# Two transformer blocks on one core: routing on unscaled rows, three weight loads issued earlier, the first expert's gate and up products apart

## The reference, cut to what matters

```python
hn = rmsnorm(h, norm_ffn[i])
tokens = hn.reshape(-1, d)
g_logits = tokens @ w_router_group
g_probs = jax.nn.softmax(g_logits, axis=-1)
g_idx = jnp.argmax(g_logits, axis=-1)
g_w = jnp.take_along_axis(g_probs, g_idx[:, None], axis=1)
e_logits = jnp.einsum("nd,gde->nge", tokens, w_router_expert)
e_sel = jnp.take_along_axis(e_logits, g_idx[:, None, None], axis=1)[:, 0]
top_v, top_i = lax.top_k(e_sel, TOP_K_IN_GROUP)
gates = g_w * jax.nn.softmax(top_v, axis=-1)
...
def run_block(args):      # xb: the tokens of expert e
    xb, e = args
    return (jax.nn.silu(xb @ w_gate[e]) * (xb @ w_up[e])) @ w_down[e]
...
out = jnp.zeros((n, d), jnp.float32).at[row_token].add(ys * row_gate[:, None])
```

## Time and profile before

| | |
|---|---|
| median of 3 runs | 996.39 us (995.67 to 996.49) |
| profiled execution, its own time | 996.21 us |
| its span, first to last instruction | 994.5 us |
| PE busy, of the span | 795.2 us (80%) |
| VectorE busy | 476.2 us (48%) |
| ScalarE busy | 315.8 us (32%) |
| mean DMA rate over the span | 289 GB/s |
| mean granted clock of TensorE | 0.918 |

### The profile page before, as it was taken

One profiled execution on the slowest core, in us unless ns is written; L12 is line 12 of the kernel. 1 busy time (PEld: TensorE's weight loads), 2 busy tenths in 40 slices (PEclk: granted clock), 3 DMA queues, 4 the chain that ended last, 5 costly groups with the idle time before them and its releaser, 6 DMA issues.

```text
span 994.5 us, 15637 instructions
## 1 busy us (share of the span) xinstructions
PE 795.2 (80%) x6490; PEld 604.5 (61%) x6490; DVE 476.2 (48%) x823; ACT 315.8 (32%) x513; POOL 90.2 (9%) x111
## 2 busy tenths in 40 slices
PE   6999999998946475646636566577998999999996
PEld 6989998775624243333413334244887888888884
DVE  5856849555322031312203122125747687766775
ACT  6754355631100000000000000004485454444443
POOL 1039554100000000000000000000001010000000
PEclk9999999999988687878879798689999999999998
DMA  9984334458999999999999999999852556555101
GB/s 306 315 289 165 129 127 170 150 203 342 383 426 426 430 427 424 430 426 426 426 426 428 427 426 426 428 426 389 283 168 87 176 184 189 209 196 169 43 2 42
DMA packets 70773, 287.00 MB, mean 289 GB/s; under 512 B 11521, under 2 KB 36398, under 8 KB 58414
## 3 DMA queue, kind: packets, MB, share of 16 engines
q1 hardware_dynamic: 70386, 285.38, 72.9%
q10 hardware_dynamic: 316, 0.58, 0.2%
HBM read 284.90 MB, written 1.05 MB: 288 GB/s over the span
## 4 chain that ended last, share of the span: by engine, by line
DMA 36%; PE 33%; issue 21%; DVE 4%; POOL 3%; ACT 3%; SPq 0%; POOLq 0%; DVEq 0%; ACTq 0%
DMA down_a<-in_w_down_dram 29%; PE bank L575 12%; PE bank L624 5%; PE bank L2072 5%; DMA pair_d<-in_w_up_dram 4%; PE bank L603 3%; PE bank L2055 2%; DMA ring<-in_w_down_dram 2%; PE bank L2045 1%; DVE act_p L522 1%; DVE w_lo L560 1%; PE bank L1902 1%; ACT w_hi L550 1%; POOL seg_r L860 1%; PE bank L612 1%
## 5 line engine op out<-in xcount | busy, mean ns | idle before, releaser
L560 DVE TENSOR_TENSOR w_lo<-ring,w_hi 128x1024 fp32r<-128x1024 f32 x137 | 176.8, 1291 | 118.7 <-ACT w_hi L550 118.5
L550 ACT ACTIVATE w_hi<-ring 128x1024 fp32r<-128x1024 f32 x138 | 146.1, 1059 | 186.6 <-PE bank L575 65.0
L575 PE MATMUL bank<-act_p,w_hi 128*128 128x256 f32 x736 | 141.1, 293 | 8.0 <-issue 7.7
L1610 DVE COPY y_e<-bank 32x256 f32<-32x256 f32 x64 | 27.2, 424 | 239.0 <-PE bank L2072 238.6
L575 PEld LDWEIGHTS bank<-act_p,w_hi 128*128 128x128 f32 x736 | 118.4, 197 | 10.7 <-issue 9.9
L591 PE MATMUL bank<-act_p,w_hi 128*128 128x512 f32 x352 | 122.0, 397 | 0.0
L1118 ACT ACTIVATE y_e<-bank 32x256 f32<-32x256 f32 x64 | 23.9, 374 | 283.3 <-PE bank L2072 282.9
L575 PE MATMUL bank<-act_p,w_lo 128*128 128x256 f32 x368 | 106.1, 288 | 0.0
L2072 PE MATMUL bank<-down_a,h_t 128*32 128x256 f32 x512 | 44.8, 509 | 71.0 <-DMA down_a<-in_w_down_dram 59.7
L2055 PE MATMUL bank<-ring,x_t 128*32 128x256 f32 x1536 | 94.2, 400 | 8.8 <-issue 8.0
L624 PE MATMUL bank<-w_hi,act_q 128*128 128x512 f32 x304 | 95.3, 394 | 0.4 <-issue 0.4
(11 more groups left out here) (356 smaller groups left out, 1032.4 us busy)
## 6 DMA issues: line engine op xcount, KB each, us to landing
ring<-in_w_up_dram SPq DMA_DIRECT2D x24, 2048.0 KB, 35.5
ring<-in_w_gate_dram SPq DMA_DIRECT2D x24, 2048.0 KB, 31.0
down_a<-in_w_down_dram SPq DMA_DIRECT2D x16, 2048.0 KB, 26.1
ring<-in_w_in_dram SPq DMA_DIRECT2D x15, 2048.0 KB, 18.8
down_b<-in_w_down_dram SPq DMA_DIRECT2D x15, 2048.0 KB, 26.1
ring<-in_w_ffn_in_dram SPq DMA_DIRECT2D x22, 1024.0 KB, 6.8
pair_d<-in_w_gate_dram SPq DMA_DIRECT2D x8, 2048.0 KB, 30.1
pair_d<-in_w_up_dram SPq DMA_DIRECT2D x8, 2048.0 KB, 34.9
```

What stands on the lines that cost most here:

```text
L550: nc.scalar.activation(parts(w_hi, g, view), view, ACT.Copy).then_inc(split_hi, 1)
L560: engine.tensor_tensor(parts(w_lo, g, view), view, h, ALU.subtract).then_inc(split_lo, 1)
L575: mm = nc.tensor.matmul(dst, parts(wt, g, grans[g][1])[:, k, :], a[:, x_part, k, :], start=(k == 0 and i == 0), stop=(k == KC - 1 and i == 2))
L1610: ins = nc.vector.tensor_copy(y_e[CAP * e:CAP * (e + 1), 256 * j:256 * (j + 1)], bank[2][CAP * j:CAP * (j + 1), 0:256])
```

## The change

1. **Router on unscaled rows.** TensorE transposes `res` itself, one block after the other, reading every eighth number of a row for a chunk (`by_feature(res)`), and writes four chunks to one PSUM bank. Two copies by ScalarE and two by VectorE, 512 columns each, take them to `tok_t`. The gain goes into the router's weights beforehand (POOL, 128 x 288 numbers). Since a positive factor per token changes no choice, the rows' scale is used only in the exponentials of the gates. The scaled rows `tok` are still made, now both blocks by ScalarE, beside the rest.
2. **Another chain.** The best and second expert are sought in all four groups at once, beside the search for the group. The conversions to whole numbers and back are gone. Gates and rounds (`gates`, `rounds`, `gate_weights`) stand later, behind the first expert's columns.
3. **First expert apart.** Its 32 columns are gathered on their own (`gather_first(0, CAP, ...)`) from a small one-hot made straight from its ranks; `gate_up_apart` makes first all gate products, then all up products; then the other 96 columns are gathered.
4. **Idle products.** Before the transposes none instead of five, after the logits four instead of five, after the ranks two instead of four.
5. **Loads.** `down_a` no longer shares its place with the routing's tables (they lie in `y_e`), and is loaded behind the pair of expert 0. The gate half of expert 3 is loaded after 56 pieces instead of 60. The gain of the final norm (`fgain`) no longer waits for the routing. The gate half of expert 4 is loaded when the gate products of expert 0 are done (`gate_read`); the loads of experts 4 to 7 are written out in front of the loop.
6. Semaphores of two small copies are merged, and the number of rounds is read from memory after two groups instead of before the first.

The core of the diff:

```diff
+    down_a = sb("down_a", [P, UNIT], where=ph)
...
+    TOK_BANK = ((4, 5), (7, 0))
+    LOGIT_BANK = (6, 1)
...
-        def load_expert(i, used, e, e_down):
-
+        def load_expert(i, used, e, e_down, gate_first=False):
+
+            if gate_first:
+                sp.wait_ge(gate_read, 1)
+                load_half(i, 0, e)
             sp.wait_ge(gu_raw, used)
-            load_half(i, 0, e)
+            if not gate_first:
+                load_half(i, 0, e)
             load_half(i, 1, e)
             sp.wait_ge(ye_raw, used)
             load_down(i, e_down)
...
             sp.wait_ge(split_hi, last_gran[u] + 1)
             sp.wait_ge(split_lo, last_gran[u] + 1)
             load_half(i, n, i)
+            if (i, n) == (0, 1):
+                sp.wait_ge(sc_sum, KC)
+                sp.wait_ge(silu_done, XC)
+                sp.wait_ge(v_used, KC)
+                load_down(0, 0)
+            if (i, n) == (2, 1):
+                sp.wait_ge(gran_used, G_WO + 12)
+                load_half(3, 0, 3)
         sp.wait_ge(gran_used, GA)
-        load_half(3, 0, 3)
         load_half(3, 1, 3)
         load_down(1, 1)
-        sp.wait_ge(routed, 1)
-        load_down(0, 0)
         sp.dma_start(fgain[:, :], w["final_norm"].partition_broadcast(P)).then_inc(ld_fgain, 16)
-        with sp.Fori(1, NE // 4) as j:
+        for i in range(4):
+            load_expert(i, i + 1, 4 + i, 2 + i, i == 0)
+        with sp.Fori(2, NE // 4) as j:
...
+        nc.gpsimd.tensor_tensor(w_rt[:, :, :], w_rt[:, :, :], bcast(g_ffn[:, :].unsqueeze(2), [P, KC, NG + NE]), ALU.mult)
...
+        nc.scalar.activation(tok[:, 0, :], res[:, 0, :], ACT.Square, accum_out=sm[:, 0:1])
+        act.wait_ge(tok_turned, 1)
+        nc.scalar.activation(*turned_out(0, 0), ACT.Copy).then_inc(tok_act, 1)
+        act.wait_ge(tok_turned, 4)
+        nc.scalar.activation(*turned_out(1, 1), ACT.Copy).then_inc(tok_act, 1)
+        act.wait_ge(res_mix, 2)
+        nc.scalar.activation(tok[:, 1, :], res[:, 1, :], ACT.Square, accum_out=sm[:, 1:2]).then_inc(ss_act, 1)
+        act.wait_ge(rstd_ready, 2)
+        act.wait_ge(ss_act, 2)
+        for b in range(TB):
+            ins = nc.scalar.activation(by_chunk(tok[:, b, :], True), by_feature(res[:, b, :], True), ACT.Copy,
+                                       scale=sm[:, 4 + b:5 + b])
+        ins.then_inc(nrm_act, 1)
...
+        for b, h in ((0, 1), (1, 0)):
+            dve.wait_ge(tok_turned, 2 * b + h + 1)
+            nc.vector.tensor_copy(tok_t[:, 4 * h:4 * h + 4, b * P:(b + 1) * P],
+                                  bank[TOK_BANK[b][h]][:, :].rearrange("p (c t) -> p c t", c=4)).then_inc(tok_dve, 1)
...
-            ins = nc.vector.tensor_copy(lgt[:, b, :], bank[6 + b][:, 0:NG + NE])
+            dve.wait_ge(logits_raw, b + 1)
+            nc.vector.tensor_copy(by_group(G_LOGIT)[:, b, :], bank[LOGIT_BANK[b]][:, 0:NG])
+            ins = nc.vector.tensor_copy(rt[:, 10, b, :], bank[LOGIT_BANK[b]][:, NG:NG + NE])
+            if b == 0:
+                dve.wait_ge(ss_act, 2)
+                nc.vector.tensor_scalar(sm[:, 2:4], sm[:, 0:2], 1.0 / D, EPS, ALU.mult, ALU.add).then_inc(ms_ready, 1)
...
+        nc.vector.tensor_reduce(g_top, by_group(G_LOGIT), AX_X, ALU.max)
+        link_dve(dve, nc.vector.tensor_reduce(groups(TOP_1), experts(10), AX_X, ALU.max))
+        nc.vector.tensor_tensor(by_group(G_EQ), by_group(G_LOGIT), by_token(g_top, NG), ALU.is_equal)
+        link_dve(dve, nc.vector.tensor_tensor(experts(0), experts(10), of_group(groups(TOP_1)), ALU.is_equal))
...
+        link_dve(dve, nc.vector.tensor_tensor(experts(3), experts(9), of_group(groups(G_HOT)), ALU.mult))
         nc.vector.tensor_tensor(rt[:, 4, :, :], rt[:, 2, :, :], rt[:, 3, :, :], ALU.add).then_inc(member, 1)
...
+        first_rank = r8[:, 9, :, 0]
+        link_dve(dve, nc.vector.tensor_copy(first_rank, bank[5][:, 0:TB * NE].rearrange("p (b e) -> p b e", b=TB)[:, :, 0]))
+        for b in range(TB):
+            ins = nc.vector.tensor_scalar(onehot[:, 1, b, 0:CAP], iota_f[:, 0:CAP], r8[:, 9, b, 0:1], rt[:, 4, b, 0:1],
+                                          ALU.is_equal, ALU.mult)
+        ins.then_inc(member, 1)
...
+            if before is None:
+                keep_first(0)
...
+            if before is None:
+                keep_first(1)
+                gates()
+                rounds()
+                gate_weights()
+                dve.wait_ge(routed, 1)
...
+        def keep_first(half):
+            dve.wait_ge(xt_raw, half + 1)
+            nc.vector.tensor_tensor(
+                x_t[:, 0, 4 * half:4 * half + 4, 0:CAP],
+                bank[(6, 1)[half]][:, 0:4 * CAP].rearrange("p (c j) -> p c j", c=4),
+                bcast(g_ffn[:, 4 * half:4 * half + 4].unsqueeze(2), [P, 4, CAP]), ALU.mult).then_inc(xt_kept, 1)
...
-        keep_running(5)
-        pe.wait_ge(res_mix, 2)
-        pe.wait_ge(nrm_act, 2)
-        pe.wait_ge(nrm_dve, 2)
-        for c in range(KC + 2):
-            if c < KC:
-                if c >= 4:
-                    pe.wait_ge(*((tok_act, (c - 4) // 2 + 1) if c % 2 == 0 else (tok_dve, (c - 5) // 2 + 1)))
-                for b in range(TB):
-                    mm = nc.tensor.transpose(bank[c % 4][:, b * P:(b + 1) * P], tok[:, b, c * P:(c + 1) * P],
-                                             ident[:, :])
-                mm.then_inc(tok_turned, 1)
-            if c >= 2:
-                k = c - 2
-                pe.wait_ge(tok_act if k % 2 == 0 else tok_dve, k // 2 + 1)
-                for b in range(TB):
-                    mm = nc.tensor.matmul(bank[6 + b][:, 0:NG + NE], tok_t[:, k, b * P:(b + 1) * P],
-                                          w_rt[:, k, :], start=(k == 0), stop=(k == KC - 1))
-        mm.then_inc(logits_raw, 1)
-        keep_running(5)
+        for b in range(TB):
+            pe.wait_ge(res_mix, b + 1)
+            for c in range(KC):
+                mm = nc.tensor.transpose(bank[TOK_BANK[b][c // 4]][:, (c % 4) * P:(c % 4 + 1) * P],
+                                         by_feature(res[:, b, :], True)[:, :, c], ident[:, :])
+                if c % 4 == 3:
+                    mm.then_inc(tok_turned, 1)
+        pe.wait_ge(const_ready, 3)
+        for b in range(TB):
+            for c in range(KC):
+                if c % 4 == 0:
+                    pe.wait_ge(tok_act if b == c // 4 else tok_dve, b + 1)
+                mm = nc.tensor.matmul(bank[LOGIT_BANK[b]][:, 0:NG + NE], tok_t[:, c, b * P:(b + 1) * P],
+                                      w_rt[:, c, :], start=(c == 0), stop=(c == KC - 1))
+            mm.then_inc(logits_raw, 1)
+        keep_running(4)
 
         pe.wait_ge(const_ready, 4)
         pe.wait_ge(member, 1)
         nc.tensor.matmul(bank[5][:, 0:NE], m_lt[:, :], rt[:, 4, 0, :], start=True, stop=True)
-        for o, last in ((NE, m_lt), (2 * NE, ones)):
-            nc.tensor.matmul(bank[5][:, o:o + NE], ones[:, :], rt[:, 4, 0, :], start=True, stop=False)
-            mm = nc.tensor.matmul(bank[5][:, o:o + NE], last[:, :], rt[:, 4, 1, :], start=False, stop=True)
-        mm.then_inc(rank_raw, 1)
-        keep_running(4)
-
-
-        pe.wait_ge(routed, 1)
-        n_more = pe.value_load(rounds_i[0:1, 2:3], min_val=NE // 8 - 1, max_val=NE // 8 * (T // CAP) - 1)
+        for dst, last in ((bank[5][:, NE:2 * NE], m_lt), (bank[7][:, 0:NE], ones)):
+            nc.tensor.matmul(dst, ones[:, :], rt[:, 4, 0, :], start=True, stop=False)
+            nc.tensor.matmul(dst, last[:, :], rt[:, 4, 1, :], start=False, stop=True).then_inc(rank_raw, 1)
+        keep_running(2)
...
+        def gather_first(o, n, banks, which):
+
+            for c in range(KC):
+                for b in range(TB):
+                    mm = nc.tensor.matmul(banks[c // 4][:, (c % 4) * n:(c % 4 + 1) * n], tok[:, b, c * P:(c + 1) * P],
+                                          onehot[:, which, b, o:o + n], start=(b == 0), stop=(b == TB - 1))
+                if c % 4 == 3:
+                    mm.then_inc(xt_raw, 1)
+
+        def gate_up_apart(e):
+            for n in range(2):
+                pe.wait_ge(*pair_landed(e, n, 1))
+                gu = PAIR[e][:, n, :].rearrange("p (k n) -> p k n", k=KC)
+                for c in range(KC):
+                    if c % 4 == 0:
+                        pe.wait_ge(xt_kept, c // 4 + 1)
+                    for j in range(4):
+                        mm = nc.tensor.matmul(bank[GU_BANK[e % 2]][CAP * j:CAP * (j + 1), n * P:(n + 1) * P],
+                                              x_t[:, 0, c, CAP * e:CAP * (e + 1)], gu[:, c, j * P:(j + 1) * P],
+                                              start=(c == 0), stop=(c == KC - 1))
+                mm.then_inc(gu_raw if n else gate_read, 1)
...
         def group_pe(k, before, s):
-            pe.wait_ge(xt_kept, 2 * k + 2)
-            gate_up_pe(k, s, 0)
+            if before is not None:
+                pe.wait_ge(xt_kept, 2 * k + 4)
+                gate_up_pe(k, s, 0)
```

(8 more changed lines are left out.)

220 lines of the change are left out of this document (115 added, 105 removed).

## The result

The changed kernel takes 982.51 us (median of 981.12 to 983.65), the kernel before 996.03 us in the same comparison; the ratio is 0.9862, interval 0.9842 to 0.9883. That is 13.5 us less, 11.7 to 15.7 by the interval. The forecast was 987.0 with a range from 985.0 to 991.5: the direction was right, the gain was half as large again as forecast, and the time lies outside the range.

A forecast was written before the change was run, and what follows sets the result against it. The prediction took the experts to be bound by DMA bytes: a stream worth a full-rate one from 242.0 instead of 251.3 gains 9.3 us, 996.21 to 986.9, plus 0.2 for the median, stated as 987.0; range 985.0 to 991.5.

The forecast's parts named there:

- What bounds the kernel: Experts: they end when their bytes have been moved by DMA, at about 427 GB/s, 4.9 us per half or down matrix.
- transposes done: Router: 16 transposes of unscaled rows start on TensorE at 219.35 and take 2.3 us, done at 221.6.
- members: Routing choice on VectorE: 14 linked steps instead of 21, 4.2 us instead of 4.93, done at 229.7.
- small gather: Expert 0's 32 columns on TensorE: bound by weight loads, 3.5 us, from 232.7 to 236.2.
- gate half issued: Expert 4's first load: issued at 238.3, after expert 0's gate products, taken as 1.9 us, end at 238.1.
- first down load issued: Expert 2's down matrix: waits for expert 0's down product, done at 250.0, and is issued at 250.2.
- rival B: Slower small steps: strided transposes double (2.3 us) or halves cost 1.8 more each; 989.3, 990.6, or 993 with both; chance 0.20.
- second gap: Stream near 250: the down load comes after both halves are done, so a second slow start, about 2 us DMA idle.
- rival C: The gap closes: expert 0's down product 1.6 us sooner or the second start free, giving 985.0; chance 0.07.
- early loads: Before the routing: DMA has 7 us free for 4.9; if `down_a` were still loaded after routing, 4.9 us would be lost.
- The step that failed: Experts' stream: same bytes in both kernels and the same 427 GB/s to the end, so no gain beyond its earlier start.
- rival E: TensorE's clock falls to 0.50 at the transposes and stays, doubling 25.5 us of work on the path: 1012; chance 0.05.

The follow-up runs named there:

- shifted version: The kernel before with 324 long-reached waits, 162 instructions, on TensorE in the second group of experts, nothing of the change in it; 992.51 us, ratio 0.9966.
- 24 or 48 further: The changed kernel with 48 or 96 long-reached waits, 24 or 48 instructions, on TensorE ahead of the loop over the experts; 984.15 and 985.82 us.
- 8 instructions nearer: The changed kernel without the two idle products between the ranks and the small gather; 982.78 us, ratio 0.9868.
- 193 nearer: The changed kernel with one gather of 128 columns, expert 0's gate and up products together, both halves loaded behind them; 986.60 us, ratio 0.9913.
- 96 further: The changed kernel with 192 long-reached waits, 96 instructions, on TensorE in the second group of experts; 985.46 us, ratio 0.9914.
- 162 nearer: The kernel before, unchanged, whose loop lies 162 instructions nearer to the program's start than the changed kernel's; 996.03 us.
- 64 nearer: The changed kernel with one gather of 128 columns instead of 32 first and 96 later, expert 0's halves still apart; 986.60 us, ratio 0.9906.
- 192 further: The changed kernel with 384 long-reached waits, 192 instructions, on TensorE in the second group of experts; 983.88 us, ratio 0.9888.

## Where the prediction was right and where it failed

**What bounds the kernel** was right: each of the stream's starts moved the end by as much, down to 1.6 us in the version with the down product first.

**The steps up to the first issue**, in the prediction's times (the changed kernel's own lie 0.97 earlier throughout, since its mixer did):

| step | forecast | measured + 0.97 |
|---|---|---|
| transposes done | 221.6 | 221.4 |
| logits done | 225.4 | 225.0 |
| members | 229.7 | 229.1 |
| small gather | 232.7 to 236.2 | 232.2 to 235.8 |
| gate half issued | 238.3 | 237.8 |
| up half issued | 240.2 | 239.5 |
| first down load issued | 250.2 | 249.3 |

Each term was right or a little high, and the sum of small excesses is 0.5 us at the gate half and 0.9 at the down load; together with a slightly better start this makes 10.27 of 9.3. The largest was the copy in front of expert 1: 0.43 us of waiting, not 0.78, for 384 columns in 0.56 us instead of 512 in 0.69. The half that was priced with a row of 128-column products cost 1.85, forecast 1.9.

**The strided transposes (rival B)** cost nothing on the path: 16 in 2.10 us with their tail, forecast 2.3, doubled 4.6. Their weight loads are recorded at 190 ns (median), where those of the kernel before, reading in order, took 143, but the products start every 0.11 us in both, so the longer loads are hidden. The rule of the Trainium skill (SBUF — State Buffer, Door 1: The DMA port swizzle), that a step of more than four fp32 numbers pays, did not decide the time here: at a step of eight the trace has no doubling.

**The second gap** was forecast at 2 us and is there; the version that closes it gained 1.6. So rival C, whose 985.0 is the nearest to the measured time, is not what happened. **The early loads** were right for `down_a` in direction, but "4.9 us would be lost" was 3.3, since a third matrix in hand closes the gap. For the fourth expert's gate half the prediction named no price; it is zero.

**The step that failed** is one sentence: "All bytes of that stream are the same in both kernels", with "then the same 427 GB/s to the end". The bytes of the loads are the same; the instructions fetched beside them are not. The kernel before had its loop in a bad place, the changed one, by the 162 instructions that the change happens to add ahead of it, in a good one. This is worth 2.7 us in the traces and 3.3 in the medians of the kernel before and its shifted version. The page of before had the row, 56 packets on the instruction queue; the prediction did not use it, and from before's trace alone the 10 could not have been told. That is the larger part of the 4.5 us by which the forecast was too high. The rest is the excess of 1.0 in the second stretch and the scatter of the clock. Without the loop's place the time would have been some 985.2 to 985.8 (an estimate, 982.51 with the 2.7 or the 3.3 added), just inside the range.

**The clock (rival E)** was put at 0.05 because it "was 0.50 only after some 6 us of nothing". This was read from too few windows. In the kernel before TensorE idles 1.97 us in the mixer and the clock then falls to 0.50 for three us (the row of 106.00 to 107.00, above); the changed kernel idles as long within 0.4 us of the same place and keeps 1.00. TensorE, before and after:

```profile
104.30 0.47 PE L575 MATMUL bank<-act_p,w_hi 128*128 128x256 f32 x2 [1.97 <-issue]
```

```profile
104.66 0.47 PE L571 MATMUL bank<-act_p,w_hi 128*128 128x256 f32 x2 [1.97 <-issue]
```

```profile
106.00:107.00 1.00, 1.00 (x10) 1.00 (x9) 1.00 (x2) 0.00 (x0) 0.00 (x0) 1.00 0.66 139
```

The piece behind it took 4.60 us instead of 3.10. Three such idle times stand in every profile: 1.97 us near 104, 2.4 near 165, 1.91 near 750. After them the clock was low in 5, 15 and 10 of the 16 profiles. The profiles in which it stayed high after the last one have 313.5 to 314.1 us from the last down product to the end, otherwise 314.8 to 316.9. These are the first and the last row of the table of stretches, 2.1 us of the 15.1 that belong to the two executions and not to the change, and without them 13.0 are left, near the 13.5 of the medians. In six of the fourteen profiles of the changed kernel and its versions the clock also fell behind the logits, for some 3 us, which made the first issue up to 0.7 later; in the shifted kernel before it was at 0.50 from 227 to 235, and the first halves were issued 3 us later than in the kernel before. So rival E's mechanism exists, at a few us and not at 25.

## What to carry to other kernels

A change that adds or takes instructions ahead of a long loop can move the loop's time by itself: compare the packets of the instruction queue in the same window of both traces before crediting the difference to the edit, and put some idle instructions ahead of the loop, in steps up to the 256 of a piece (24 or 48 further were enough here to spoil some executions, 64 or 162 to mend a bad place). The stream of loads broke here unless the next load was issued in time before the last one in hand was done (1.7 us was too little, 2.8 us enough); count loads in hand at each place where one depends on computed data, and bring the releasing product forward instead of making everything faster. And a mark or two (here an issue in the mixer and the last down product) that cut both spans into stretches show at once what share of a difference lies outside the change.

## What the runs showed of the chip

**The loop's code.** The loop has 1,752 instructions on TensorE (428 products, nearly all of two matmul records and two weight loads, and some 50 others). It ran two passes of some 118 us (eight experts of three matrices at 4.9) without a packet, or was fetched anew in each, depending on the number of instructions ahead of it, and as far as these runs tell on that number modulo 256. The changed kernel's place and 8 instructions nearer were good. 24 and 48 further were good in the one execution profiled of each, while other executions took 3 to 5 us more; 193 nearer, which is 63 further within a piece, fetched in one of the two passes. 96 further was bad, and 162 nearer, which is 94 further within a piece, too; so were 64 nearer and 192 further, which are the same place. The Trainium skill (Runtime: NRT & Kernel Launch, Instruction fetch mechanics) gives 128 KiB for TensorE's instructions, refilled in blocks of 16 KiB or 256 instructions. The block agrees with 10 packets of 0.16 MB and with the equality of 192 further and 64 nearer. In the same section the Trainium skill calls this memory a FIFO, filled in sequence, with no instruction cache; here the trace disagrees, since two passes of seven blocks each fetched nothing.

**The clock.** Idle times of 1.9 to 2.4 us were followed by the lower level in some executions of the same kernel's code and not in others; expert 0's gate and up products ran low in both profiles without idle products ahead of the gather and in none of the twelve with them (nine of these have the same narrow gather and halves).

**The start of a load.** From an idle queue the full rate came 2 to 3 us after the issue; with 1.7 us of lead part of that showed, with 2.8 us none.
